# Attention heads and head norms moved into the value projection of a decoder layer, output projection split in two halves

## The reference, cut to what matters

```python
proj = u @ w_in           # hq, hf, hi, hg (HGRN2 heads) and sq, sk, sv (stick-breaking heads), 8 heads of 128 each
o_h = rms_norm(hgrn2_chunked(...), hg_norm) * silu(hg)
z = q . k * SCALE + bias                         # per head, keys before the query only
log_1mb = where(mask, log_sigmoid(-z), 0)
later = cumsum(log_1mb, reverse) - log_1mb
a = where(mask, exp(log_sigmoid(z) + later), 0);  o_s = rms_norm(a @ v, sb_norm)
mix = concat(o_h, o_s) @ w_o
x = layer_norm(ALPHA * x + g1 * mix, ln1_g, ln1_b)
u2 = x * (1 + sc2) + sh2
x = layer_norm(ALPHA * x + g2 * hier_moe(u2))    # top-1 group, then top-2 of its experts
```

## Time and profile before

| | us |
|---|---|
| median of 3 runs | 1871.92 (1866.95 to 1881.08) |
| profiled execution, its own time | 1872.5 |
| its span | 1870.7 |
| mean granted TensorE clock | 0.935 |
| TensorE busy | 1638.1 (88%) |
| VectorE busy | 533.5 (29%) |
| ScalarE busy | 178.4 (10%) |
| GpSimd busy | 128.8 (7%) |

### The profile page before, as it was taken

How to read it: one execution, slowest core, us unless ns; L and a number is a source line. 1 busy time by engine, 2 the same in 40 slices (tenths; PEclk the granted TensorE clock), 3 DMA queues, 4 the chain that set the end, 5 groups by cost and what they waited for, 6 DMA issues and landing times.

```text
span 1870.7 us, 24750 instructions
## 1 busy us (share of the span) xinstructions
PE 1638.1 (88%) x9583; PEld 957.2 (51%) x9583; DVE 533.5 (29%) x882; ACT 178.4 (10%) x274; POOL 128.8 (7%) x158
## 2 busy tenths in 40 slices
PE   3679999999999999679977999999889888898971
PEld 0046666546787844557763554545444444454430
DVE  0010029702212212540026223232222222323218
ACT  0000010200000010330006100000000000000002
POOL 3000000001101100010011100000000000000004
PEclk8689999999979899879998799999999999999985
DMA  9998888874424255243342599999999999999951
GB/s 354 421 384 314 314 322 328 311 296 157 149 91 135 97 198 184 99 163 133 113 158 96 214 415 410 411 414 421 412 400 416 398 414 411 402 422 414 415 214 50
DMA packets 78909, 536.41 MB, mean 287 GB/s; under 512 B 10257, under 2 KB 10433, under 8 KB 17425
## 3 DMA queue, kind: packets, MB, share of 16 engines
q1 hardware_dynamic: 72146, 507.62, 68.3%
q0 software_dynamic: 6384, 25.83, 4.3%
q10 hardware_dynamic: 336, 2.36, 0.3%
HBM read 532.87 MB, written 11.80 MB: 291 GB/s over the span
## 4 chain that ended last, share of the span: by engine, by line
PE 33%; DMA 12%; DVE 5%; issue 2%; SPq 2%; ACT 1%; DVEq 0%; ACTq 0%
PE ps L1023 13%; DMA ring<-w_gate 11%; PE ps L899 7%; PE ps L1043 6%; PE ps L1005 2%; SPq L358 2%; DMA arena<-w_down 2%; DVE arena L1764 1%; PE ps L977 1%; PE ps L1011 1%; ACT arena L1235 1%; PE ps L913 0%; DVE arena L1635 0%; PE ps L891 0%; PE ps L890 0%
## 5 line engine op out<-in xcount | busy, mean ns | idle before, releaser
L1023 PE MATMUL ps<-ring,arena 128*64 128x256 f32 x3200 | 360.9, 384 | 24.9 <-DMA ring<-w_gate 22.8
L583 PE MATMUL ps<-arena,ring 128*128 128x288 f32 x1280 | 322.8, 411 | 0.0
L1023 PEld LDWEIGHTS ps<-ring,arena 128*64 128x64 f32 x3200 | 230.6, 138 | 171.0 <-DMA ring<-w_gate 35.7
L583 PEld LDWEIGHTS ps<-arena,ring 128*128 128x128 f32 x1280 | 241.3, 191 | 90.2 <-issue 25.5
L1043 PE MATMUL ps<-arena 128*64 128x512 f32 x800 | 179.9, 599 | 21.0 <-DVE arena L1775 17.6
L567 PE MATMUL ps<-ring,silu_c 128*32 128x512 f32 x768 | 116.3, 717 | 53.6 <-DMA ring<-w_ada 27.2
L899 PE MATMUL ps<-arena,ring 128*128 128x288 f32 x512 | 128.7, 411 | 9.7 <-DVE arena L1603 9.7
L1005 PE MATMUL ps<-arena 64*128 64x512 f32 x400 | 110.3, 649 | 23.0 <-DVE arena L1764 14.7
L1043 PEld LDWEIGHTS ps<-arena 128*64 128x64 f32 x800 | 65.3, 137 | 118.8 <-issue 109.4
L899 PEld LDWEIGHTS ps<-arena,ring 128*128 128x128 f32 x512 | 98.6, 193 | 37.8 <-DVE arena L1603 10.2
L591 PE MATMUL ps<-ring,arena 128*128 128x512 f32 x256 | 113.4, 596 | 1.3 <-ACT arena L1083 1.3
(11 more groups left out here) (395 smaller groups left out, 1247.2 us busy)
## 6 DMA issues: line engine op xcount, KB each, us to landing
ring<-w_gate SPq DMA_DIRECT2D x100, 1024.0 KB, 22.9
ring<-w_up SPq DMA_DIRECT2D x100, 1024.0 KB, 25.7
arena<-w_down SPq DMA_DIRECT2D x100, 1024.0 KB, 25.8
ring<-w_ada SPq DMA_DIRECT2D x96, 1024.0 KB, 8.3
ring<-w_in SPq DMA_DIRECT2D x56, 1024.0 KB, 6.3
ring<-w_o SPq DMA_DIRECT2D x16, 1024.0 KB, 4.9
ring<-cache_k SPq DMA_DIRECT2D x16, 512.0 KB, 4.0
ring<-cache_v SPq DMA_DIRECT2D x16, 512.0 KB, 4.2
```

The costliest lines, as they stand in the source:

```text
L583: last = mm(ps[:, bank, 0:T], ring[:, slot, P * t:P * (t + 1)], uT[:, t, :], start=(t == 0), stop=(t == KC - 1))
L1023: last = mm(ps[B * s:B * (s + 1), 2 + c // 4, 0:256], xgT[:, 4 * (c % 4) + t, :], ring[:, c, 512 * t + 256 * s:512 * t + 256 * (s + 1)], s ...
```

## The change

In the value projection the first four chunks of weights are cut into halves, and the keys of a sequence come after each half, so all eight sequences are done after four chunks. The last four chunks are cut into halves too, and after each of these eight halves one step of the head loop is issued: the sum of squares for one HGRN2 head (line 848 of the changed kernel), the scores of one stick-breaking head, and the cumulative sums of the head before. The sample attention lies in the same eight steps. The products with v (`head_out`) come after the last step. The order of the loads is changed to match (`sv_order`).

The HGRN2 heads are normalised one at a time inside the steps (`head_square`, `scale_head`). The first half of each of the output projection's first four chunks, which needs the HGRN2 heads alone, is issued before the stick-breaking heads are normalised; the sums of squares for these (line 948) lie between.

VectorE adds up rT and its squares for the LayerNorm (`add_sums`), and TensorE sums the result over the rows once, at the end. The factor ALPHA is taken out of x: g1 is divided by it, and the LayerNorm's epsilon by its square, so GpSimd's pass over x goes away, as does its square. GpSimd loads x when the last chunk of the value projection is used.

The updates of the HGRN2 state are issued in pairs on two groups of 32 rows, into two PSUM banks. Several areas of SBUF change places.

The core of the diff (areas of memory, waits of the other engines and the load order's details are left out):

```diff
-                    if 8 * half + c >= 1:
-                        pe.wait_ge(u_dve, 8 * half + c)
-                    tt, r0 = c // 4, CH * (c % 4)
-                    for h in range(4):
-                        k = heads[h]
-                        last = mm(ps[:, 2, P * h:P * (h + 1)], kdt[r0:r0 + CH, tt, h, :], ...
                     if c % 2 == 0:
+                        if 8 * half + c >= 1:
+                            pe.wait_ge(u_dve, 8 * half + c)
+                        tt = c // 4
+                        for h in range(4):
+                            k = heads[h]
+                            for c2 in range(2):
+                                r0 = CH * (c % 4 + c2)
+                                last = mm(ps[:, (2, 6)[c2], P * h:P * (h + 1)], kdt[r0:r0 + CH, tt, h, :], ...
...
+            for c in range(4):
+                n = SV["w", c]
+                pe.wait_ge(slot_loaded[n % SLOTS], loaded(n))
+                row_half(n % SLOTS, c, 0)
+                key_pages(2 * c)
+                row_half(n % SLOTS, c, 1)
+                key_pages(2 * c + 1)
+            for s in range(H):
+                c = 4 + s // 2
...
+                row_half(n % SLOTS, c, s % 2)
+                pe.wait_ge(hsq_act, s + 1)
...
+                mm(ps[:, 3, 0:T], ones[:], sqh[s % 2], start=True, stop=True).then_inc(hm_pe, 1)
...
+                mm(z[:, 0:256], skT[:, s, 0:128], sqT[:, s, 0:256], start=True, stop=True)
+                mm(z[:, 256:384], skT[:, s, 128:256], sqT[:, s, 128:256], start=True, stop=True
+                   ).then_inc(z_pe, 1)
+                if s >= 1:
+                    cumulate(s - 1)
+                if s == 1:
...                                  # scores of the new sample tokens
+                if s == 3:
+                    pe.wait_ge(ss_dve, 2)
+                    pe.wait_ge(hln_act, 4)
...                                  # cumulative sums of the sample tokens
+                if s == 5:
+                    pe.wait_ge(ss_act, 2)
+                    past_values(0)
+                    past_values(1)
+                if s == 6:
+                    past_values(2)
+                    past_values(3)
+            for b in range(4, NSEQ):
+                past_values(b)
...
+            cumulate(H - 1)
...                                  # head_out(0) to head_out(7)
+            pe.wait_ge(hm_dve, H)
+            for m in range(4):
...
+                wo_half(m, 0)
+                if m < 2:
+                    pe.wait_ge(nsq_act, m + 1)
...
+                    for k in range(4):
+                        last = mm(ps[:, k, 0:T], ones[:], sqs[:, 4 * m + k, :], start=True, stop=True)
+                    last.then_inc(nm_pe, 1)
+            pe.wait_ge(nm_dve, 2)
             for m in range(KC):
...
+                    wo_half(m, 0)
+                wo_half(m, 1)
+            pe.wait_ge(acc_dve, 2 * (KC - 1))
+            mm(ps[:, 2, 0:T], ones[:], mu, start=True, stop=True)
+            mm(ps[:, 3, 0:T], ones[:], lt1, start=True, stop=True).then_inc(st_pe, 1)
...
+            def add_sums(m):                                   # VectorE
+                dve.wait_ge(wo_act, m + 1)
+                if m >= 2:
+                    dve.wait_ge(acc_dve, 2 * (m - 1))
+                v.tensor_tensor(mu, mu if m >= 2 else rT[:, 0, :], rT[:, m, :], ALU.add).then_inc(acc_dve, 1)
+                v.tensor_tensor(lt1, lt1 if m >= 2 else r2[0], r2[m % 4], ALU.add).then_inc(acc_dve, 1)
...
                 if h >= 1:                                     # ScalarE, loop over the heads
                     k = h - 1
                     act.wait_ge(d_dve, k + 1)
...
+                    A(aa[k], zn[k % 2], ACT.Exp).then_inc(a_ready, 1)
+                if h + 1 < H:
+                    head_square(h + 1)
                 if h == 1:
                     act.wait_ge(ss_dve, 1)
...
-            nc.gpsimd.tensor_tensor(sqo[0], hout, hout, ALU.mult).then_inc(nsq_pool, 1)
...
-            nc.gpsimd.tensor_scalar(xa, xa, ALPHA, 0.0, ALU.mult, ALU.add).then_inc(xa_ready, 1)
```

More of the change, by code:

```diff
@@ L109, in layer @@
         uT = area(0, KC, T)
-        mixT = uT
+        mixT = area(9216, KC, T)
         SQ = 4608
@@ L300, in loaded @@
         def loaded(n):
-            def pages_of(m):
-                return N_V <= m < N_WO or (N_SV <= m < N_V and (m - N_SV) % 2 == 1)
-            return 16 * sum(2 if pages_of(m) else 1 for m in range(n % SLOTS, n + 1, SLOTS))
+            return 16 * sum(2 if m in page_chunks else 1 for m in range(n % SLOTS, n + 1, SLOTS))
         @block.sync
@@ L338, in put_pages @@
                                  ).then_inc(slot_loaded[n % SLOTS], 16)
-            for c in range(SLOTS):
-                put(N_SV + 2 * c + 1, 2 * c % SLOTS, w_in[6, c])
-                put_pages(N_SV + 2 * c + 1, c, cache_k)
-            for b in range(NSEQ):
-                put_pages(N_V + b, b, cache_v)
+            for kind, i in sv_order:
+                n = SV[kind, i]
+                if kind == "w":
+                    put(n + 1, n % SLOTS, w_in[6, i])
+                else:
+                    put_pages(n, i, cache_k if kind == "K" else cache_v)
             with sp.Fori(0, 2) as g:
@@ L587, in row_chunk, with row_half @@
             def row_chunk(slot, c):
-                for t in range(4):
+                row_half(slot, c, 0)
+                row_half(slot, c, 1)
+            def row_half(slot, c, part):
+                for t in (2 * part, 2 * part + 1):
                     for i, (t0, tn) in enumerate(TILES[0:2]):
@@ new lines, in _ @@
+                    past_values(1)
[4 more added lines that the diff above has]
+                past_values(b)
+            for k in range(H):
+                i, j = k // 4, k % 4
+                last = mm(ps[32 * j:32 * j + 32, 7, P * i:P * (i + 1)], aN[:, k, :], tok[0:TS, 2, P * k:P * (k + 1)],
+                          start=False, stop=(i == 1))
+                if k == 3:
+                    pe.wait_ge(parts_dve, 2)
+                    fold_parts(parts_sv)
+                    pe.wait_ge(evac_dve, 24)
@@ new lines, in _, with wo_half @@
+            for k in range(4):
+                head_out(k)
+            pe.wait_ge(ss_dve, 4)
+            for i in range(2):
+                last = nc.tensor.transpose(ps[:, 7, 256 + P * i:256 + P * (i + 1)], orow[:, i, :], ident[:])
+            last.then_inc(ss_pe, 1)
+            pe.wait_ge(d_dve, H)
+            pe.wait_ge(hln_act, H)
+            pe.wait_ge(a_ready, H)
+            for k in range(4, H):
+                head_out(k)
+            def wo_half(m, part):
+                n = N_WO + m
+                for k in range(8 * part, 8 * part + 8):
+                    last = mm(ps[:, 4 + m % 4, 0:T], ring[:, n % SLOTS, P * k:P * (k + 1)], mixT[:, k, :],
+                              start=(k == 0), stop=(k == KC - 1))
+                if part == 1:
+                    last.then_inc(ring_used, 1)
@@ L897, in _ @@
                     pe.wait_ge(wo_dve, m - 3)
-                for k in range(KC):
-                    last = mm(ps[:, 4 + m % 4, 0:T], ring[:, n % SLOTS, P * k:P * (k + 1)], mixT[:, k, :],
-                              start=(k == 0), stop=(k == KC - 1))
-                last.then_inc(ring_used, 1)
-                if m >= 2:
-                    sums(m - 2)
-            sums(KC - 2)
-            sums(KC - 1)
+                    wo_half(m, 0)
+                wo_half(m, 1)
+            pe.wait_ge(nln_act, 2)
@@ L1554, in _ @@
                     v.tensor_tensor(n, x, negmask[:], ALU.add)
+                if h >= 1:
+                    scale_head(h - 1)
+                if h == H - 1:
+                    dve.wait_ge(ring_used, used(SV["w", 7]))
+                    v.tensor_copy(parts_sv, ps[:, 6, :]).then_inc(parts_dve, 1)
+                    for i in range(2):
+                        v.tensor_copy(tok[:, i, 512:1024], ps[:, 4 + i, :])
+                if h < H:
                     dve.wait_ge(soft_act, h + 1)
@@ new lines, in _ @@
+            for j in range(2, 4):
+                dve.wait_ge(o_pe, j + 1)
+                v.tensor_copy(mixT[:, H + 2 * j:H + 2 * j + 2, 0:TP], ps[:, j, :].rearrange("p (h t) -> p h t", h=2)
+                              ).then_inc(o_dve, 1)
+            link(v.tensor_scalar(adaT[:, 2], adaT[:, 2], 1.0 / ALPHA, None, ALU.mult))
+            for half in range(2):
+                dve.wait_ge(nrs_act, half + 1)
+                dst = mixT[:, H + 4 * half:H + 4 * half + 4, :]
+                v.scalar_tensor_tensor(dst, dst, normw[:, 1:2], rst[:, 4 * half:4 * half + 4, :], ALU.mult, ALU.mult
+                                       ).then_inc(nm_dve, 1)
```

416 lines of the change are left out of this document (206 added, 210 removed).

## The result

The changed kernel took **1822.7 us** (median of 4 runs, 1821.21 to 1825.11) against 1869.4 us for the kernel before on the same chip. The ratio is 0.975, with a 95% interval from 0.972 to 0.978. The profiled execution took 1822.23 us, with a span of 1820.5 us (before 1872.5 and 1870.7). The forecast was 1822 us.

The account below looks back on a forecast made before the run. Bound: a cross-engine head chain leaving TensorE idle. The value-to-LayerNorm stretch falls from 318.0 to 270.2 us; 1872.5 - 47.8 - 7 (paired updates) + 4 (clock) = 1821.7, predicted 1822 us; range 1809 to 1842 us, leaving out 2 in 10 runs.

Parts of the forecast that it names:

- The bound: Head loop and norms: a chain through TensorE, VectorE and ScalarE leaves TensorE busy 51.4 of 82 us.
- First half of the value projection: Value projection's first four chunks with eight page pairs and seven score pairs: 55.8 us, with no stall.
- The eight steps: Head loop interleaved with the value projection's second half, through products with v and transposes: 82.4 us in total.
- The four us charged: Clock loss on TensorE: some 2 us each for gaps in step 3 and for past values at the end.
- the second place in the forecast: Past values at the end of the head loop, where the granted clock was expected to fall: some 2 us.
- The output projection and the norms: Output chunks and stick-breaking norm sums 128.0 us, plus 4.0 us from last matmul to VectorE's first LayerNorm instruction.
- State updates in pairs: HGRN2 state updates on two 32-row groups: 7 us saved, bounds nothing and 9.2 us.
- The prediction's 1.7 us for a pair: HGRN2 state updates: 16 weight loads at 0.107 us if loads in two groups did not overlap, a gain of 4.7 us.
- Cold steps: Rival, head-loop steps: small gaps keep the clock at 1.2 GHz, 25 to 35 us more, 1843 to 1857 us; chance 0.14.
- The chain is longer than its parts: Rival, head loop: semaphore waits add 1 us per step and squares come late, about 1835 us; chance 0.10.
- Slower: Rival: clock stays at 1.2 GHz from step 0 into the output projection, 1883 us; chance 0.03.
- The expert stage: Rival: expert loads go 1% slower, costing 7.7 us, 1829 us, instead of the stage only moving; chance 0.03.

Follow-up runs that it names:

- norms first: Changed kernel, edited so the output projection starts only after the norms of the stick-breaking heads: 1829.5 us, ratio 0.977 to the kernel before.
- filler run: Changed kernel plus ten unused matmuls in TensorE's gap before the fourth head-loop step's sum of squares: 1820.4 us, ratio 0.974 to the kernel before.

## Why the prediction was right, step by step

**The bound.** Right. The head loop was idle time of TensorE, and it went where the prediction put it: the run with the steps behind the weights gives 22.9 us and norms first 8.9, against 32.5 us that the stretch became shorter. The two runs cut at different places, so their sum is no proof that nothing else is in it.

**First half of the value projection.** Forecast 55.8 us, measured 56.2 (644.35 to 700.5), with no idle row in it.

**The eight steps.** The table has the end of each step's scores, as the start of the next row, counted from 700.5 us.

| step | 0 | 1 | 2 | 3 | 4 | 5 | 6 | 7 | output projection |
|---|---|---|---|---|---|---|---|---|---|
| forecast | 9.7 | 15.4 | 22.1 | 33.4 | 44.7 | 51.5 | 59.3 | 67.9 | 82.4 |
| measured | 10.1 | 15.9 | 22.2 | 35.4 | 49.8 | 56.4 | 64.4 | 73.1 | 87.1 |

Steps 3 and 4 are 5.0 us over the forecast; the three steps ahead add 0.1 and all that is behind gives 0.4 back. The two waits there were forecast at 4.5 and 2.1 us and were 5.27 and 1.55, put down to ScalarE as said. The rest is the clock, which the prediction charged in a term of its own. By the rows above, in step 3 the sum of squares with the scores took 2.40 us (733.45 to 735.85) for 1.19 in step 2. The sample's sums took 5.33 (738.91 to 744.24), and in the filler run 3.45 (737.64 to 741.09). The four us charged were therefore about right for this profile (4.5 by the filler run), but the place was half wrong: all of it lies behind the gap of step 3, none behind the past values. In the other profiles of the same code the clock cost up to 3 us more. In one of them, without alternation, it did fall once behind the past values, to 0.50 from 780.6 to 784.0 us, where a product with v took 1.06 us in place of 0.60:

```profile
781.71 1.06 PE L904 MATMUL ps<-arena 128*128 128x256 f32 x2
```

So the second place in the forecast was possible, and it was luck that this profile had neither that nor the longer cold stretch.

**The output projection and the norms.** Forecast 132.0 us, measured 132.1. The tail was forecast at 4.0 us and is 3.9. The forecast's split of its own sum was off, though: it gave the LayerNorm's sums 15 us, where the run shows 11.7, as three pairs had stood in the tail before and the new tail is longer. It gave the norms 12; the run with the norms first shows 8.9, but it leaves the HGRN2 heads' norms in the steps, and what moving those gave no run shows. The sum was made from the new rows, not from the split, so it did not suffer. (Its terms behind step 7 add up to 82.2 us and not 82.4, and those of the loop to 6.7 and not 6.6, which changes nothing.)

**State updates in pairs.** Forecast 7 us, within 0 to 9.2; measured 8.6. This is the term that was mis-sized: the reading of the combination's rows (39% saved) was too low. It was also taken for one effect and is two, half from issuing two chunks together and half from alternating the row groups.

In one group the passes of 128 columns start 0.112 us apart (576.79, 576.91 and 577.02 us before the change). Alternated, each group keeps that pace and the other group's pass starts 0.007 us behind, so 16 passes leave 0.07 us for each. The Trainium skill ("TensorE: Matmul & The Clock Gate", LDWEIGHTS) gives 0.107 us for a weight load of 128 columns. The trace is near that within one group, but can't tell the load from the pass itself: passes of 288 and 512 columns take 0.24 and 0.44 us, which would be an estimated 0.11 us for 128 columns. The prediction's 1.7 us for a pair whose loads do not overlap is near the 1.63 us without alternation by chance, since the two groups did overlap there, as the starts of the passes show. The Trainium skill ("TensorE: Matmul & The Clock Gate", Part 3, The mechanism) says that a weight load overlaps matmuls in flight only when its row group differs. The trace agrees that loads overlap across groups, but not with the "only". The passes of 288 columns use all rows and each has a load of its own; they follow each other at 0.24 us and those of 512 at 0.44, about in the ratio of their columns, which leaves no time for a load between them.

**The rivals.** *Cold steps* did not happen: the clock was 0.94 over the whole stretch, and 1.00 once the gap of step 3 was short. The Trainium skill ("TensorE: Matmul & The Clock Gate", A second HAM failure mode) tells of frequent short idle times, from which the prediction called this rival the likely case by that page. The trace doesn't test it: the stretch had six idle rows in 87 us (0.67 to 5.27 us), and the clock fell only behind the two in step 3, of 5.27 and 1.55 us. In the filler run, with the first of them closed, it did not fall behind the second either, though that had grown to 1.98 us. The rival is real, though, and the run with the steps behind the weights shows it: about 1.3 us for the sum of squares in five of the eight steps, and gaps of over 3 us. *The chain is longer than its parts*: no, the first three steps end within 0.5 us of the forecast. *Slower*: the clock came back within step 4 (by 750.3 us when the change ran again). *The expert stage*: 824.6 us for 825.4, it only moved.

**What cancelled.** The total is within 1 us partly by luck. The terms sum up as: stretch of the value and output projections +1.2 us over the forecast (275.4 for 270.2 + 4), state updates -1.7, the part ahead of them -1.4, which nothing in the change touches, experts -0.8, and the LayerNorm to the experts +3.3. The last was not forecast. That its code is unchanged was taken to mean that its time is too. The luck is also in the profile: when the changed kernel ran again, its profiled span was 1824.4 us, 3.9 us longer, with 278.1 us for the two stretches in place of 275.4. The medians of the two, 1822.7 and 1823.5 us, are what the forecast hits.

**Still open.** Why the clock falls some 1 to 3 us earlier in the stretch of 76 us than in that of 73. The kernels without alternation and with norms first have the change's code in that stretch, and show 73. Its starting time differs between them, but no run varied that alone. Open too is why the clock stays low for longer behind step 3's gap in some profiles.

## What to carry to other kernels

When a chain across engines leaves TensorE idle, put a piece of independent matmul work as long as the chain's round trip between its links, and then look for the one link that is longer: here a fill of zeros in front of it cost at least 8.6 us, half of it through the clock behind the gap. Take the length of a stretch from more than one profile where the clock falls in it: the same steps took 143.3 to 146.3 us here. Work whose result is not yet needed and that another engine can do at leisure, as that fill on GpSimd or a running sum on VectorE, goes off the chain whole. Predict such a change from the start times of the new order, row by row, and keep the clock as a term with a place of its own, so that a filler of unused matmuls can test it.

## What the runs showed of the hardware that was not expected

- Two groups of 32 rows, alternated pass by pass, take 16 passes of 128 columns in 1.09 us, the time of 8 in one group (1.08). Eight in one group and then eight in the other take 1.63, since the second group starts before the first has issued its last pass.
- Ten unused matmuls of 288 columns in a gap of 5.3 us kept the clock at 1.00 in place of 0.73, and made the program's stretch 4.5 us shorter.
- The stretch with the steps, with one gap of 5.3 us in it, took 143.3, 144.9, 145.0 and 146.3 us in four profiles of the same code, at a granted clock of 0.96, 0.94, 0.94 and 0.93.
- A stretch of unchanged code, with TensorE idle for a third of it, had one of two lengths, 73 or 76 us, and a kernel that was run again kept its own. The whole difference is TensorE's busy time (49.0 or 52.1 us).
- A fill of 128 x 4096 zeros takes 3.52 us on GpSimd and 3.47 on VectorE.
